# Stick-breaking attention of a two-block model: two heads walked in step, and the sum over later key blocks kept as one

## The chip, the cores and the metric

The kernel runs on one core of a Trainium2 chip. The metric is the device time of one launch in microseconds (us), the median over runs. Four engines do the arithmetic, each with a queue of its own that it works through strictly in the order in which the program wrote it: TensorE (PE) multiplies matrices, VectorE (DVE) and ScalarE (ACT) work element by element and read PE's results from PSUM, GpSimd (POOL) works on SBUF. They wait for one another by semaphores.

## The reference

Two transformer-like blocks run one behind the other on 512 tokens of width 1024 (528 in the second, which puts 16 meta tokens in front). The change touches only the mixer of the second block. That mixer has two halves which share nothing but their input and output projections.

The first half is stick-breaking attention with 8 heads of width 64. Positions are padded to 640, five key blocks of 128:

```
z = q·k * scale
log_keep = where(valid, -softplus(z), 0)            # valid: key before query
log_rest = sum of log_keep over the later keys, own key excluded
attn = where(valid, exp(log_sigmoid(z) + log_rest), 0);  out = attn @ v
```

The second half is a delta-rule recurrence with 8 heads of width 64: S = S·diag(w) + sa(kk·a)^T + v k^T, y = S r. The kernel evaluates it in 9 chunks of 64 positions. Each chunk needs a triangular inverse of its own, and then a step that depends on the state of the chunk before.

## The kernel before, in words

Both halves run interleaved. In the kernel each engine's part is a set of Python generators; at every `yield` another generator may write its next instructions, and `alternate(...)` decides the order. So the order on each engine is fixed when the program is written. A step of a generator is called a tick here.

**The recurrence** is the generator `rk`. It has `rw_prepare(n)` (products of the chunk, L865 and L873, transposes L878/L879, then the inverse: some 14 small steps of 64x64 matmuls, L596 and L615, each answered by a copy or an addition on DVE or ACT of about 0.4 us) and `rw_scan(n)` (L897/L898 "r", L906 "x", L914 "sd", L919/L923 "y"). Two prepares and one scan are under way at a time, in three turns. On PE `rk` has 250 ticks in all (counted from the code).

In "r", the product AR·SB (128 rows, 64 columns of weights, L897) and the product MM·V0 (L898) are added in PSUM. V0 is a tile with 128 rows: its upper 64 rows are zero and its lower 64 rows are the chunk's values, which POOL copies there from SV (L2219) for each of the 9 chunks. The copy waits for every mask and product of POOL before it, and POOL's later operations wait for the copy.

**The attention** is `heads(b)`, once for b = 0 and once for b = 1; each works on 4 heads (i = 0 to 3). The two halves of the partitions, rows 0 to 63 and rows 64 to 127, hold the heads of b = 0 and of b = 1. For each head it walks the key blocks j = 4, 3, 2, 1, 0, whose query widths are `LEN` = 128, 256, 384, 512, 512 (x counts them 0 to 4). For one block:

- PE: z = KA·QA, one fp32 matmul with 64 rows (L938; each fp32 matmul is two records in the profile)
- ACT: abs, exp, ln (L2003, L2005, L2007)
- DVE: softplus as max(z, 0) + ln (L1538); the block at j = 0 is also multiplied by a mask of the padding (L1543)
- POOL: zero above the diagonal (L2098)
- ACT: the negated value, rounded to fp32r, into `KHI` at the block's own place (L2011); DVE: what rounding left over, into `KLO` (L1546)
- PE: into the same PSUM bank add `TRIR` times this block and `ONER` times every block with a larger j, each for the high and the low part (L947). So a head's five blocks have 2, 4, 6, 8 and 10 of these matmuls
- ACT: exp, which gives the attention weights (L2015); POOL: mask (L2098)

After five blocks PE multiplies the weights by V (L955, 5 matmuls with 128 rows and 64 columns, two records each), and ACT copies the result (L2018).

One head takes 26 ticks of `heads(b)` (104 for four heads). The order is `alternate(rk, heads(0), rk, later_by(2, heads(1)))`: in each round two ticks of `rk` and one of each `heads`. DVE and ACT also run `attention_parts()`, which after `ATT_TICKS` rounds prepares the attention's result for the output projection.

After the last of both halves SP loads the first four weights of the output projection and reloads the residual (XSAVE) and the bonus term (BON). The group norm and the output projection (L489) follow.

Of the kernel before, what the change touches and what calls it, by code (L numbers as in the profile page):

```python
# [15 lines left out]
NCH = 9  # L16
ATT_TICKS = 107
# [129 lines left out]
def program(nc, xT, metaT, cols, consts, slabs, lup, gup, out):  # L147
# [137 lines left out]
    V0 = sbuf("V0", [128, 8, 64], st=m4)  # L285
# [87 lines left out]
    rz = steps("rz", "v0", "sb")  # L373
# [4 lines left out]
    rv0 = count("rv0")  # L378
# [9 lines left out]
    hg = [steps(f"hg{i}", "mask", "emask") for i in range(2)]  # L388
    cat2_hi, cat2_lo = count("cat2_hi"), count("cat2_lo")
# [37 lines left out]
    BLOCKS = (4, 3, 2, 1, 0)  # L427
    KHI = [HH[:, a:a + 4, :].rearrange("p k t -> p (k t)") for a in (0, 4)]
# [48 lines left out]
    def tensor():  # L477
# [407 lines left out]
        def rw_scan(n):  # L885
            e, t = n % 2, n // 2
            te.wait_ge(*rv0.at(n))
            if n:
                te.wait_ge(*qd.at("w1", n - 1))
                if n > 1:  # L890
                    te.wait_ge(*qm.at(n - 2))
            else:
                te.wait_ge(*rz.at("sb"))
# [23 lines left out]
            if n:  # L917
                for i in range(4):
                    te.matmul(PS[:, 6, 64 * i:64 * i + 64], SB[:, i, :, :].rearrange("p a t -> p (a t)"),  # L919
                              AR[:, i, n, 1, :], start=True, stop=True)  # L920
                    for par in range(2):
                        h = 2 * i + par
                        ins = te.matmul(PS[64 * par:64 * par + 64, 6, 64 * i:64 * i + 64], SV[e][:, h, :],  # L923
                                        MM[e][:, h, 64:128], start=False, stop=True, skip_group_check=True)
                ins.then_inc(*qy.up(n - 1))
            yield

        def heads(b):
            pb = 64 * b
            for i in range(4):  # L930
                h = 2 * i + b
                for x, j in enumerate(BLOCKS):
                    r, n = 5 * i + x, LEN[j]
                    if x:
                        te.wait_ge(*ha[b].at("att", r - 1))
                    elif i:
                        te.wait_ge(*hs[b].at(i - 1))
                    te.matmul(PS[:, b, 0:n], KA[pb:pb + 64, i, 128 * j:128 * j + 128], QA[pb:pb + 64, i, 512 - n:512],  # L938
                              start=True, stop=True).then_inc(*hp[b].up("z", r))
                    yield  # L940
                    yield
                    yield
                    te.wait_ge(*hd[b].at("lo", r))
                    for q in range(4, j - 1, -1):
                        w = TRIR if q == j else ONER
                        for part in (KHI[b], KLO[b]):
                            ins = te.matmul(PS[:, b, n - LEN[q]:n], w[:, :], part[:, OFF[q]:OFF[q] + LEN[q]],  # L947
                                            start=False, stop=True, skip_group_check=True)
                    ins.then_inc(*hp[b].up("c", r))
                    yield  # L950
                    yield
                te.wait_ge(*ha[b].at("att", 5 * i + 4))
                te.wait_ge(*hg[b].at("emask", 4 * i + 3))
                for j in range(5):
                    ins = te.matmul(PS[pb:pb + 64, b, 512 - LEN[j]:512], VT[:, j, 64 * h:64 * h + 64],  # L955
                                    ATT[b][:, OFF[j]:OFF[j] + LEN[j]], start=(j == 0), stop=(j == 4))
                ins.then_inc(*ho[b].up(i))
                yield

        te.wait_ge(*rz.at("v0"))  # L960
# [3 lines left out]
        rk = pipeline(NCH, rw_prepare, rw_scan)  # L964
        alternate(rk, heads(0), rk, later_by(2, heads(1)))
# [46 lines left out]
    def vector():  # L1012
# [518 lines left out]
        def heads(b):  # L1531
            for i in range(4):
                for x, j in enumerate(BLOCKS):
                    r, n = 5 * i + x, LEN[j]
                    t = TT[b][r % 2]
                    yield
                    ve.wait_ge(*ha[b].at("ln", r))
                    ve.scalar_tensor_tensor(t[:, 0:n], PS[:, b, 0:n], 0.0, t[:, 0:n], ALU.max,  # L1538
                                            ALU.add).then_inc(*hd[b].up("m", r))
                    if j == 0:  # L1540
                        ve.wait_ge(*hd[b].at("m", r))
                        ve.wait_ge(*fz.at("pm"))
                        ve.tensor_scalar(t[:, 0:n], t[:, 0:n], PM[:, 0:1], None, ALU.mult).then_inc(*hm[b].up(i))  # L1543
                    yield
                    ve.wait_ge(*ha[b].at("hi", r))
                    ve.scalar_tensor_tensor(KLO[b][:, OFF[j]:OFF[j] + n], t[:, 0:n], -1.0,  # L1546
                                            KHI[b][:, OFF[j]:OFF[j] + n].bitcast(f32), ALU.mult,
                                            ALU.subtract).then_inc(*hd[b].up("lo", r))
                    yield
                    yield  # L1550
                    yield
                yield

# [9 lines left out]
        ve.wait_ge(*rz.at("v0"))  # L1563
        ve.wait_ge(*rz.at("sb"))
        for s in s_bs:
            ve.wait_ge(s, 16)
        rk = pipeline(NCH, rw_prepare, rw_scan)
        alternate(rk, heads(0), rk, later_by(2, heads(1)), attention_parts())
# [42 lines left out]
    def scalar():  # L1611
# [382 lines left out]
        def heads(b):  # L1994
            pb, a = 64 * b, ha[b]
            for i in range(4):
                for x, j in enumerate(BLOCKS):
                    r, n = 5 * i + x, LEN[j]
                    t = TT[b][r % 2][:, 0:n]
                    ae.wait_ge(*hp[b].at("z", r))  # L2000
                    if r >= 2:
                        ae.wait_ge(*hd[b].at("lo", r - 2))
                    ae.activation(t, PS[:, b, 0:n], ACT.Abs).then_inc(*a.up("abs", r))  # L2003
                    ae.wait_ge(*a.at("abs", r))
                    ae.activation(t, t, ACT.Exp, scale=-1.0).then_inc(*a.up("exp", r))  # L2005
                    ae.wait_ge(*a.at("exp", r))
                    ae.activation(t, t, ACT.Ln, bias=1.0).then_inc(*a.up("ln", r))  # L2007
                    yield
                    yield
                    ae.wait_ge(*(hg[b].at("mask", 4 * i + x) if j else hm[b].at(i)))  # L2010
                    ae.activation(KHI[b][:, OFF[j]:OFF[j] + n], t, ACT.Copy, scale=-1.0).then_inc(*a.up("hi", r))  # L2011
                    yield
                    yield
                    ae.wait_ge(*hp[b].at("c", r))
                    ae.activation(ATT[b][:, OFF[j]:OFF[j] + n], PS[:, b, 0:n], ACT.Exp).then_inc(*a.up("att", r))  # L2015
                    yield
                ae.wait_ge(*ho[b].at(i))
                ae.activation(QA[pb:pb + 64, i, :], PS[pb:pb + 64, b, :], ACT.Copy).then_inc(*hs[b].up(i))  # L2018
                yield

# [12 lines left out]
        rk = pipeline(NCH, rw_prepare, rw_scan)  # L2033
        alternate(rk, heads(0), rk, later_by(2, heads(1)), attention_parts())
# [46 lines left out]
    def gpsimd():  # L2081
# [113 lines left out]
        ge.memset(V0[0:64, :, :], 0.0).then_inc(*rz.up("v0"))  # L2195
        ge.memset(SB[:, :, :, :], 0.0).then_inc(*rz.up("sb"))

        def after_copy():
            if rv0.n:
                ge.wait_ge(*rv0.at(rv0.n - 1))  # L2200

        def rw_prepare(n):
# [5 lines left out]
            after_copy()  # L2208
            yield from invert(rinv[e], rd[e], rg[e], t, False)

        def rw_scan(n):
            e, t = n % 2, n // 2
            ge.wait_ge(*ra[e].at("v", t))
            if n:
                ge.wait_ge(*qp.at("r", n - 1))
            for s in hg + rg:
                if s.n:
                    ge.wait_ge(s.sem, s.n)
            ge.tensor_copy(V0[64:128, :, :], SV[e][64:128]).then_inc(*rv0.up(n))  # L2219
# [4 lines left out]
        def heads(b):  # L2224
            for i in range(4):
                for x, j in enumerate(BLOCKS):
                    r = 5 * i + x
                    yield
                    if j:
                        after_copy()  # L2230
                        ge.wait_ge(*hd[b].at("m", r))
                        keep_above(TT[b][r % 2][:, 0:128]).then_inc(*hg[b].up("mask", 4 * i + x))
                    yield
                    yield
                    yield
                    if j:
                        after_copy()
                        ge.wait_ge(*ha[b].at("att", r))
                        keep_above(ATT[b][:, OFF[j]:OFF[j] + 128]).then_inc(*hg[b].up("emask", 4 * i + x))
                    yield  # L2240
                yield

        rk = pipeline(NCH, rw_prepare, rw_scan)
        alternate(rk, heads(0), rk, later_by(2, heads(1)))


# [212 lines left out]
```

## Time and profile before

| | |
|---|---|
| median of 3 runs | 2175.62 us (2174.77 to 2176.39) |
| the profiled execution | 2179.63 us |
| its span | 2178.4 us |
| PE busy in the span | 2005.8 us (92%) |
| DVE, ACT, POOL busy | 789.1, 706.8, 762.8 us |

"Busy" is the time in which an engine has an instruction in it. Matmuls overlap, so for PE the distance from one start to the next says more than the duration. "Granted clock" is the share of TensorE's full 2.4 GHz that the chip allowed; at 0.5 it runs at 1.2 GHz. The mixer of the second block, with the recurrence and the attention, lies between 1428 and 1726 us of the span.

### The profile page before, as it was taken

What the parts mean: (1) busy time and instruction counts of PE and PEld (TensorE: products, weight loads), DVE (VectorE), ACT (ScalarE), POOL (GpSimd) and SP (SyncE); (2) the same over time, 40 slices, a digit from 0 to 9 for tenths busy, and PEclk for the clock granted to TensorE, in tenths of its full rate; (3) what the DMA queues carried; (4) which work ended last, traced back from release to release, by engine and by line L of the source; (5) the groups of instructions that cost most, each with busy time, mean ns of one, the idle gap of its engine ahead of it and who ended that gap; (6) DMA issues with size and microseconds to landing.
All of it is one profiled execution on the core that took longest, in us unless ns stands there. A gap on an engine that the chain in (4) does not pass through costs nothing. (4 is left out here: it accounts for less than half of the span.)

```text
span 2178.4 us, 32154 instructions
## 1 busy us (share of the span) xinstructions
PE 2005.8 (92%) x13960; PEld 1688.1 (77%) x13960; DVE 789.1 (36%) x1065; ACT 706.8 (32%) x1056; POOL 762.8 (35%) x444
## 2 busy tenths in 40 slices
PE   3879988999999999999999888888999789999997
PEld 2657767777888889999999888876666568888885
DVE  5664452232111103444310366643443433344201
ACT  2453221332322323222222323344554333222222
POOL 2322121434444554444445322211111144444453
PEclk9999998999999999999999989998998899999999
DMA  7332221323333232222233412000000222322321
GB/s 270 116 116 97 71 86 30 100 88 131 126 97 91 88 101 88 91 93 89 85 95 93 130 59 63 30 6 2 2 2 2 115 80 87 97 90 94 97 91 64
DMA packets 55659, 182.76 MB, mean 84 GB/s; under 512 B 7488, under 2 KB 7744, under 8 KB 55392
## 3 DMA queue, kind: packets, MB, share of 16 engines
q1 hardware_dynamic: 55520, 180.72, 25.6%
q8 instruction: 110, 1.80, 0.4%
q14 instruction: 29, 0.24, 0.0%
HBM read 175.45 MB, written 5.24 MB: 83 GB/s over the span
## 5 line engine op out<-in xcount | busy, mean ns | idle before, releaser
L2090 POOL TENSOR_TENSOR WL<-RAWS,WH 128x1024 fp32r<-128x1024 f32 (+2 forms) x275 | 650.4, 2368 | 991.8 <-ACT WH L1622 991.8
L489 PE MATMUL PS<-HH,WH 128*128 128x264 f32 (+2 forms) x2184 | 676.8, 352 | 48.5 <-issue 11.9
L489 PE MATMUL PS<-HL,WH 128*128 128x264 f32 (+2 forms) x2184 | 660.0, 345 | 0.0
L489 PE MATMUL PS<-HH,WL 128*128 128x264 f32 (+2 forms) x2184 | 656.3, 342 | 0.0
L489 PEld LDWEIGHTS PS<-HH,WH 128*128 128x128 f32 (+1 forms) x2184 | 382.6, 193 | 117.0 <-issue 35.6
L1622 ACT ACTIVATE WH<-RAWS 128x1024 fp32r<-128x1024 f32 (+2 forms) x275 | 284.1, 1034 | 453.3 <-PE PS L489 405.7
L489 PEld LDWEIGHTS PS<-HL,WH 128*128 128x128 f32 (+1 forms) x2184 | 383.4, 193 | 47.9 <-issue 1.9
L489 PEld LDWEIGHTS PS<-HH,WL 128*128 128x128 f32 (+1 forms) x2184 | 382.4, 192 | 49.0 <-issue 0.4
L489 PE MATMUL PS<-IHf,WH 128*128 128x512 f32 (+1 forms) x704 | 209.4, 338 | 0.0
L489 PE MATMUL PS<-IHf,WL 128*128 128x512 f32 (+1 forms) x704 | 209.3, 338 | 0.0
L489 PE MATMUL PS<-ILf,WH 128*128 128x512 f32 (+1 forms) x704 | 209.2, 338 | 0.0
L1369 DVE TENSOR_TENSOR TMP<-TMP,PS 128x512 f32<-128x512 f32 (+1 forms) x66 | 45.8, 693 | 254.0 <-PE PS L489 246.8
L1889 ACT ACTIVATE IHf<-TMP 128x512 fp32r<-128x512 f32 (+1 forms) x66 | 42.1, 638 | 285.3 <-DVE TMP L1369 285.3
L489 PEld LDWEIGHTS PS<-IHf,WH 128*128 128x128 f32 x704 | 120.5, 188 | 14.9
L489 PEld LDWEIGHTS PS<-ILf,WH 128*128 128x128 f32 x704 | 120.7, 188 | 14.8
L489 PEld LDWEIGHTS PS<-IHf,WL 128*128 128x128 f32 x704 | 120.4, 188 | 14.9
L1364 DVE TENSOR_TENSOR TMP<-TMP,RSTD 128x528 f32<-128x528 f32 (+1 forms) x44 | 104.4, 2374 | 41.2 <-ACT TMP L1885 41.2
L1376 DVE SCALAR_TENSOR_TENSOR X<-PS,X 128x528 f32<-128x528 f32 (+1 forms) x16 | 11.2, 700 | 222.5 <-PE PS L489 222.5
L1357 DVE TENSOR_TENSOR TMP<-PS,RSTD 128x528 f32<-128x528 f32 (+1 forms) x44 | 30.8, 700 | 150.8 <-PE PS L489 150.1
L2106 POOL TENSOR_TENSOR SQA<-SQA,TMP 128x512 f32<-128x512 f32 (+1 forms) x39 | 53.1, 1361 | 90.4 <-ACT TMP L1635 89.7
L1371 DVE TENSOR_TENSOR ILf<-TMP,IHf 128x512 fp32r<-128x512 f32 (+1 forms) x66 | 47.9, 726 | 46.5 <-ACT IHf L1889 46.5
L1635 ACT ACTIVATE TMP<-X 128x512 f32<-128x512 f32 (+1 forms) x42 | 26.2, 628 | 84.8 <-DVE X L1376 35.7
(493 smaller groups left out, 1929.6 us busy)
## 6 DMA issues: line engine op xcount, KB each, us to landing
RAWS<-w_w_in SPq DMA_DIRECT2D x52, 512.0 KB, 4.3
RAWS<-w_ada SPq DMA_DIRECT2D x32, 512.0 KB, 3.6
RAWS<-w_f0g SPq DMA_DIRECT2D x22, 512.0 KB, 3.5
RAWS<-w_f0u SPq DMA_DIRECT2D x22, 512.0 KB, 3.9
RAWS<-w_f1g SPq DMA_DIRECT2D x22, 512.0 KB, 3.6
RAWS<-w_f1u SPq DMA_DIRECT2D x22, 512.0 KB, 3.6
RAWS<-w_f2g SPq DMA_DIRECT2D x22, 512.0 KB, 3.6
RAWS<-w_f2u SPq DMA_DIRECT2D x22, 512.0 KB, 3.6
```

The costliest lines, as they stand in the source:

```text
L489: ins = te.matmul(ps[0:m, q, o:o + b - a] if len(halves) > 1 else ps[0:m, o:o + b - a], w[:, k * m:k * m + m], v[:, k0 + k, a:b], start=fi ...
L1357: ve.tensor_tensor(tv, place(f, 2 * j), r, ALU.mult).then_inc(*ff_g.up("g", FT * (f - 1) + j))
L1364: ve.tensor_tensor(tv, tv, r, ALU.mult).then_inc(*ff_g.up("r", FT * (f - 1) + j))
L1369: ve.tensor_tensor(tv, tv, place(f, 2 * j + 1), ALU.mult).then_inc(*ff_mul.up(FT * f + j))
L1371: ve.tensor_tensor(IL[f][:, j, :], t, IH[f][:, j, :].bitcast(f32), ALU.subtract).then_inc(*ff_lo.up(FT * f + j))
L1376: ve.scalar_tensor_tensor(xv, place(f, 2 * FT + m), 0.5 if f else MOD[:, 40 + m:41 + m], xv, ALU.mult, ALU.add).then_inc(*ff_x.up(8 * f + m))
L1622: ae.activation(WH[s % NS][:, 0:n], RAW[i % NR][:, 0:n], ACT.Copy).then_inc(*w_hi.up(s))
L1635: ae.activation((TMP[k % 3] if k else SQA)[:, 0:n], X[:, k, t0:T2], ACT.Square).then_inc(*n_sq.up(8 * SQUARED[q] + k))
L1889: ae.activation(IH[f][:, j, :], t, ACT.Copy).then_inc(*ff_hi.up(FT * f + j))
L2090: ge.tensor_tensor(WL[s % NS][:, 0:n], RAW[i % NR][:, 0:n], WH[s % NS][:, 0:n].bitcast(f32), ALU.subtract).then_inc(*w_lo.up(s))
L2106: ge.tensor_tensor(SQA[:, 0:n], SQA[:, 0:n], TMP[k % 3][:, 0:n], ALU.add).then_inc(*n_acc.up(added(q, k)[1] - 1))
```

## The change

1. `heads(0)` and `heads(1)` become one generator `heads()`, in which every step is written for b = 0 and then for b = 1. The z matmuls of the two heads stand next to each other, and so do their sums and their products with V, where the two heads alternate matmul by matmul.
2. A block now has ten ticks instead of five: abs at tick 0, exp 1, ln 2, softplus and mask 4, high part 5, low part 6, sums on PE 7, exp 8, mask of the weights 9. With a tick for the product with V a head pair has 51 ticks, 204 in all. The order becomes `alternate(rk, both, rk, both, rk, both, rk)`: four ticks of `rk` to three of `both`. `ATT_TICKS` goes from 107 to 67.
3. The blocks with a larger j are no longer multiplied one by one. POOL adds this block's log_keep to the running sum (three additions per head, 128, 256 and 384 wide), ACT rounds it (`upper_sum`), DVE takes the remainder (`lower_sum`), and PE multiplies that one sum by `ONER`. The five blocks of a head have 2, 4, 4, 4 and 4 such matmuls: 18 instead of 30.
4. V0 and its copy are gone. "r" multiplies MM[64:128] by SV[64:128], the chunk's values where they lie, with 64 rows.
5. In "y" the four matmuls of L919 come first, with the start flag on the first alone, then the eight of L923.

```diff
             for i in range(4):                                  # rw_scan, "r"
                 for par, q in enumerate(HALF):
                     te.matmul(PS[q, 6, 64 * i:64 * i + 64], AR[:, i, n, 0, :], SB[:, i, par, :], start=True, stop=False)
-                    ins = te.matmul(PS[q, 6, 64 * i:64 * i + 64], MM[e][:, 2 * i + par, 0:64], V0[:, 2 * i + par, :],
-                                    start=False, stop=True)
+                    ins = te.matmul(PS[q, 6, 64 * i:64 * i + 64], MM[e][64:128, 2 * i + par, 0:64],
+                                    SV[e][64:128, 2 * i + par, :], start=False, stop=True)
...
                 for i in range(4):                              # rw_scan, "y"
                     te.matmul(PS[:, 6, 64 * i:64 * i + 64], SB[:, i, :, :].rearrange("p a t -> p (a t)"),
-                              AR[:, i, n, 1, :], start=True, stop=True)
-                    for par in range(2):
-                        h = 2 * i + par
-                        ins = te.matmul(... SV[e][:, h, :], MM[e][:, h, 64:128], start=False, stop=True, ...)
+                              AR[:, i, n, 1, :], start=i == 0, stop=False, skip_group_check=True)
+                for h in range(8):
+                    ins = te.matmul(... SV[e][:, h, :], MM[e][:, h, 64:128], start=False, stop=True, ...)
...
+                    for b, q in enumerate(HALF):                # PE, heads
+                        te.matmul(PS[:, b, 0:n], KA[q, i, 128 * j:128 * j + 128], QA[q, i, 512 - n:512], start=True,
+                                  stop=True).then_inc(*hp[b].up("z", r))
+                    for _ in range(7):
+                        yield
+                    for b in range(2):
+                        te.wait_ge(*hd[b].at("lo", r))
                         for part in (KHI[b], KLO[b]):
-                            ins = te.matmul(PS[:, b, n - LEN[q]:n], w[:, :], part[:, OFF[q]:OFF[q] + LEN[q]], ...)
+                            ins = te.matmul(PS[:, b, 0:n], TRIR[:, :], part[:, KAT[x]:KAT[x] + n], ...)
+                        if x:
+                            if x > 1:
+                                te.wait_ge(*hl[b].at(3 * i + x - 2))
+                            m = LEN[j + 1]
+                            for part in (KHI[b], KLO[b]):
+                                ins = te.matmul(PS[:, b, n - m:n], ONER[:, :], part[:, 512:512 + m], ...)
...
                 for j in range(5):
-                    ins = te.matmul(PS[pb:pb + 64, b, 512 - LEN[j]:512], VT[:, j, 64 * h:64 * h + 64], ...)
+                    for b, q in enumerate(HALF):
+                        h = 2 * i + b
+                        ins = te.matmul(PS[q, b, 512 - LEN[j]:512], VT[:, j, 64 * h:64 * h + 64], ...)
...
+        def lower_sum(i, x, b):                                 # DVE
+            n = LEN[BLOCKS[x]]
+            ve.wait_ge(*hh[b].at(3 * i + x - 1))
+            ve.scalar_tensor_tensor(KLO[b][:, 512:512 + n], TT[b][(5 * i + x) % 2][:, 0:n], -1.0, ...)
...
+        def upper_sum(i, x):                                    # ACT, between ln and the high part
+            for b in range(2):
+                ae.wait_ge(*ht[b].at(3 * i + x - 1))
+                ae.activation(KHI[b][:, 512:512 + n], TT[b][r % 2][:, 0:n], ACT.Copy, scale=-1.0)
...
-            ge.tensor_copy(V0[64:128, :, :], SV[e][64:128]).then_inc(*rv0.up(n))
...
+                    if x in (1, 2, 3):                          # POOL, tick 7
+                        for b in range(2):
+                            t = TT[b][r % 2][:, 128:n]
+                            ge.wait_ge(*hd[b].at("lo", r))
+                            ge.tensor_tensor(t, t, TT[b][(r - 1) % 2][:, 0:n - 128], ALU.add)
...
-        alternate(rk, heads(0), rk, later_by(2, heads(1)), attention_parts())
+        alternate(rk, both, rk, both, rk, both, rk, attention_parts())
```

## Rows read from the trace of the kernel before

**Rows 1.** Windows: stretch; time; busy (x count) PE, PEld, DVE, ACT, POOL; clock; DMA.

```profile
1428.00:1684.00 256.00, 235.36 (x3016) 174.04 (x3016) 109.73 (x244) 128.07 (x285) 35.87 (x90) 0.91 0.01 2
1684.00:1726.00 42.00, 33.09 (x534) 28.14 (x533) 16.52 (x37) 8.58 (x19) 2.12 (x4) 0.84 0.01 2
```

**Rows 2.** Chain of waits behind the stage: start, length, what.

```profile
1728.55 12.99 DMA BON<-bsave
...
1750.10 19.96 PE PS L489 x76
```

**Rows 3.** The same chain inside the stage: z matmuls of four widths, one V product.

```profile
1553.26 0.42 PE PS L938 x2
...
1568.11 0.64 PE PS L938 x2
...
1580.93 0.84 PE PS L938 x2
...
1584.97 1.05 PE PS L938 x2
...
1673.88 3.16 PE PS L955 x10
```

**Rows 4.** Timeline of PE, a head's last sum: start, duration, line, shapes.

```profile
1600.49 0.33 PE L947 MATMUL PS<-HH,ONER 128*128 128x128 f32 x1 [0.41 <-DVE HL L1546]
...
1600.76 0.33 PE L947 MATMUL PS<-HH,ONER 128*128 128x256 f32 x1
...
1601.05 0.34 PE L947 MATMUL PS<-HH,ONER 128*128 128x384 f32 x1
...
1601.40 0.40 PE L947 MATMUL PS<-HH,ONER 128*128 128x512 f32 x1
...
1601.87 0.40 PE L947 MATMUL PS<-HH,TRIR 128*128 128x512 f32 x1
```

**Rows 5.** The same timeline, where lines follow one another on PE.

```profile
1602.94 0.63 PE L596 MATMUL PS<-KC,rv1XB 64*64 64x64 f32 x16
1603.41 0.63 PE L596 MATMUL PS<-rv1XB,rv1C 64*64 64x64 f32 x16
1603.97 0.34 PE L897 MATMUL PS<-SB,AR 128*64 128x64 f32 x4
...
1604.95 3.18 PE L955 MATMUL PS<-RAWS,VT 128*64 128x512 f32 x10
...
1612.72 0.69 PE L914 MATMUL PS<-X 128*64 128x64 f32 x16
1613.34 0.43 PE L919 MATMUL PS<-AR,SB 128*128 128x64 f32 x2
1613.70 0.34 PE L923 MATMUL PS<-X 128*64 128x64 f32 x4
1613.97 0.43 PE L919 MATMUL PS<-AR,SB 128*128 128x64 f32 x2
...
1621.54 1.16 PE L865 MATMUL PS<-AR,BK 64*128 64x128 f32 x16
1622.63 0.68 PE L906 MATMUL PS<-RAWS,RX 64*64 64x64 f32 x16
```

**Rows 6.** Groups by line and form, 1428 to 1726: busy, mean ns, idle before.

```profile
L897 PE MATMUL PS<-SB,AR 128*64 128x64 f32 x144 | 10.6, 240 | 2.1 <-DVE SB L1527 1.3 <-POOL V L2219 0.8
...
L1546 DVE SCALAR_TENSOR_TENSOR HL<-TMP,HH 128x512 fp32r<-128x512 f32 x12 | 9.1, 754 | 8.1 <-ACT HH L2011 8.1
...
L1538 DVE SCALAR_TENSOR_TENSOR TMP<-PS,TMP 128x512 f32<-128x512 f32 x12 | 8.2, 687 | 8.5 <-ACT TMP L2007 8.5
...
L2007 ACT ACTIVATE TMP<-TMP 128x512 f32<-128x512 f32 x12 | 7.6, 633 | 0.4
...
L2098 POOL TENSOR_SCALAR_AFFINE_SELECT TMP<-TMP 128x128 f32<-128x128 f32 x24 | 7.1, 297 | 125.0 <-DVE TMP L1538 125.0
```

**Rows 7.** The same view, whole span, POOL: an addition of two tiles.

```profile
L2106 POOL TENSOR_TENSOR SQA<-SQA,TMP 128x512 f32<-128x512 f32 x32 | 43.5, 1358 | 70.5 <-ACT TMP L1635 69.7
```

More of the change, by code:

```diff
@@ L16 @@
 NCH = 9
-ATT_TICKS = 107
+ATT_TICKS = 67
 DELTA_TICKS = 30
@@ L370, in program @@
     at_tr = count("at_tr")
-    rz = steps("rz", "v0", "sb")
+    rz = count("rz")
     rp = [steps(f"rp{i}", "bk", "u", "tr", *INV_PE) for i in range(2)]
@@ L388, in program @@
     hg = [steps(f"hg{i}", "mask", "emask") for i in range(2)]
+    ht, hh, hl = ([count(f"{x}{i}") for i in range(2)] for x in ("ht", "hh", "hl"))
     cat2_hi, cat2_lo = count("cat2_hi"), count("cat2_lo")
@@ new lines, in heads @@
+                    for _ in range(3):
+                        yield
+                for b in range(2):
+                    te.wait_ge(*ha[b].at("att", 5 * i + 4))
+                    te.wait_ge(*hg[b].at("emask", 4 * i + 3))
+                for j in range(5):
+                    for b, q in enumerate(HALF):
+                        h = 2 * i + b
+                        ins = te.matmul(PS[q, b, 512 - LEN[j]:512], VT[:, j, 64 * h:64 * h + 64],
+                                        ATT[b][:, OFF[j]:OFF[j] + LEN[j]], start=(j == 0), stop=(j == 4))
+                        if j == 4:
+                            ins.then_inc(*ho[b].up(i))
@@ L963, in tensor @@
         te.wait_ge(*at_vt.at("t1", 3))
-        rk = pipeline(NCH, rw_prepare, rw_scan)
-        alternate(rk, heads(0), rk, later_by(2, heads(1)))
+        rk, both = pipeline(NCH, rw_prepare, rw_scan), heads()
+        alternate(rk, both, rk, both, rk, both, rk)
         def joined2(k):
@@ L1544, in heads @@
-                    yield
[L1545 to L1551, printed above, removed]
-                yield
+                    for _ in range(4):
+                        yield
@@ L2007, in heads @@
-                    ae.activation(t, t, ACT.Ln, bias=1.0).then_inc(*a.up("ln", r))
+                    t = [TT[b][r % 2][:, 0:n] for b in range(2)]
+                    for b in range(2):
+                        ae.wait_ge(*hp[b].at("z", r))
+                        if x >= 2:
+                            ae.wait_ge(*ht[b].at(3 * i + x - 2))
+                        ae.activation(t[b], PS[:, b, 0:n], ACT.Abs).then_inc(*ha[b].up("abs", r))
+                    yield
+                    for b in range(2):
+                        ae.wait_ge(*ha[b].at("abs", r))
+                        ae.activation(t[b], t[b], ACT.Exp, scale=-1.0).then_inc(*ha[b].up("exp", r))
@@ L2008, in heads @@
+                    yield
+                    for b in range(2):
+                        ae.wait_ge(*ha[b].at("exp", r))
+                        ae.activation(t[b], t[b], ACT.Ln, bias=1.0).then_inc(*ha[b].up("ln", r))
+                    yield
+                    if x in (2, 3, 4):
+                        upper_sum(i, x - 1)
                     yield
                     yield
-                    ae.wait_ge(*(hg[b].at("mask", 4 * i + x) if j else hm[b].at(i)))
-                    ae.activation(KHI[b][:, OFF[j]:OFF[j] + n], t, ACT.Copy, scale=-1.0).then_inc(*a.up("hi", r))
+                    for b in range(2):
+                        ae.wait_ge(*(hg[b].at("mask", 4 * i + x) if j else hm[b].at(i)))
+                        ae.activation(KHI[b][:, KAT[x]:KAT[x] + n], t[b], ACT.Copy, scale=-1.0).then_inc(*ha[b].up("hi", r))
@@ new lines, in heads @@
+                    yield
+                    yield
+                for b, q in enumerate(HALF):
+                    ae.wait_ge(*ho[b].at(i))
+                    ae.activation(QA[q, i, :], PS[q, b, :], ACT.Copy).then_inc(*hs[b].up(i))
+                yield
+        def upper_sum(i, x):
+            r, n = 5 * i + x, LEN[BLOCKS[x]]
+            for b in range(2):
+                ae.wait_ge(*ht[b].at(3 * i + x - 1))
+                ae.activation(KHI[b][:, 512:512 + n], TT[b][r % 2][:, 0:n], ACT.Copy,
+                              scale=-1.0).then_inc(*hh[b].up(3 * i + x - 1))
@@ L2032, in scalar @@
             ae.wait_ge(s, 16)
-        rk = pipeline(NCH, rw_prepare, rw_scan)
-        alternate(rk, heads(0), rk, later_by(2, heads(1)), attention_parts())
+        rk, both = pipeline(NCH, rw_prepare, rw_scan), heads()
+        alternate(rk, both, rk, both, rk, both, rk, attention_parts())
         def group_norm(i):
```

147 lines of the change are left out of this document (65 added, 82 removed).

## The prediction

> **What bounds the kernel now.** The windows come first [rows 1]. While attention and recurrence run together, from 1428 to 1684 us, PE has work in it for 235.4 of 256 us at a granted clock of 0.91; ACT is busy for half of that time, DVE for 43%, POOL for 14%. After 1684 us only the recurrence is left: 42 us with 33.1 us of PE work at a clock of 0.84. So over the stage of 298 us PE is busy 268.5 us and idle 29.5 us. It is the bound for the first 256 us, and a chain of small steps is the bound of the last 42.
>
> The chain of waits shows next what hangs on the end of the stage: the reload of BON takes 12.99 us and the output projection starts at 1750.10 us, 24 us after the last step of the recurrence [rows 2]. SP waits for the last of both halves before it loads, before and after the change, so I carry these 24 us over. What the change is worth is then PE time, plus what the new order does to PE's idle time.
>
> **The prices on PE.** A z matmul takes 0.42, 0.64, 0.84 and 1.05 us for 128, 256, 384 and 512 columns, a V product 3.16 us [rows 3]. In a sum, two matmuls (high and low part) take, start to start, 0.27 us for 128 columns, 0.29 for 256, 0.35 for 384 and 0.47 for 512 [rows 4].
>
> Starts in [rows 5] show two more things. First, matmuls on the two halves of the array overlap: 8 of 128 columns with 64 rows, alternating halves, take 1.09 us (L865), 0.14 us each, where one alone takes 0.42 [rows 3]. Second, a change of the tile's shape costs time. Sixteen records of 64x64 take 0.47 us when the next matmuls have the same shape (1602.94 to 1603.41) and 0.56 us when the next are 128x64 (1603.41 to 1603.97): +0.09 us to leave. L914 (128x64) comes from 64x64 and goes to 128x128 and takes 0.62: about 0.04 more to enter and 0.02 of its own. L897/L898 and L955 share a shape. I take 0.13 us for one change.
>
> **Part by part**, at full clock.
>
> *z matmuls in pairs.* One head costs 0.42 + 0.64 + 0.84 + 2 x 1.05 = 4.0 us, eight heads 32.0 us. Paired as L865's are, the second is free: -16.0 us. Bounds: 0 (no overlap for long matmuls) and -16.0.
>
> *V products in pairs.* 8 x 3.16 = 25.3 us, halved: -12.6 us. Alternating 128x64 tiles are L914's form: 8 products of 64 columns in 0.62 us, 0.08 each, so they overlap too. Bounds 0 and -12.6.
>
> *One sum in place of the later blocks.* A head paid 0.27, 0.56, 0.91, 1.38 and 1.85 us, with 0.09 for leaving each time 5.4 us in all. It now pays 0.27, 0.29 + 0.27, 0.35 + 0.29, 0.47 + 0.35 and 0.47 + 0.47, together 3.23, and half of the leaving (two heads share it), 3.46 us. 8 x 1.96 = -15.7 us. Only columns and shapes enter, so I keep no wide bound here.
>
> *"y" reordered.* A group of L919 and two L923 takes 0.63 us, L919 0.36 of it [rows 5]; four make 2.5 us. Afterwards four L919 in a row, 4 x 0.32, one change and eight products as L914's 0.62: 1.95 us. -0.57 x 8 = -4.6 us.
>
> *"r" without the copy.* Here the edit costs PE time. Now sixteen products, all 128x64, take 0.98 us (1603.97 to 1604.95), because the two halves overlap. Afterwards AR·SB keeps 128 rows and MM·SV has 64, and they alternate: 16 changes of shape at 0.13 us are 2.1 us, and between two changes there is one product of two records and nothing beside it, 16 x 2 x 0.059 = 1.9 us (0.059 is 0.47 over 8). That is 4.0 us for 0.98, +3.0 us in each of 9 chunks: +27.1 us. The trace has no run of this alternation. Bounds: 0 (the change of row count counts for nothing) and +27.1; I take the upper end, since every change of row or column count that [rows 5] show was paid for. In return POOL's copy goes; PE waited 0.8 us for it in L897 [rows 6]: -0.8 us.
>
> The Trainium skill says in "TensorEngine Tiling (Array Packing)", section Tiling Modes, that changing the tiling mode, as opposed to the tile, drains the engine; it names no price. The same page's table of theoretical speedups (section Overview) gives up to a factor of two for a contraction of 64 or less, by which the new MM·SV would be the cheaper form: "r" would stay at 0.98 us or fall, and the 27.1 us would not come. The drain agrees with the 0.56 against 0.47 us; no row here shows the gain for products that all sit in the same half of the rows.
>
> *Sum on PE:* -16.0 - 12.6 - 15.7 - 4.6 + 27.1 - 0.8 = -22.6 us; at the stage's mean clock of 0.90 that is -25 us.
>
> *What moves to the others.* ACT gets 24 roundings of the running sum, at most 0.63 us each (15 us), DVE 24 remainders, at most 0.75 (18 us), POOL 24 additions, each under the 1.36 us of a 512-wide one [rows 6, 7], and loses 9 copies. Over a stage of 270 us ACT comes to about 152 us busy and DVE to 144; neither is the bound. Their cover: `upper_sum` lies on ACT after ln, while two softplus operations (0.69 each) and a mask (0.30) are under way, 1.7 us against its 1.3. Without that cover it would cost up to 15 us. POOL's additions have until the next block's ln. Behind them on POOL wait the mask of the weights, wanted only by the V product, and the inverse's two products.
>
> The trace has the remainder (two SBUF inputs, L1546) at 0.754 us and the softplus (one input in PSUM) at 0.687 [rows 6]. The Trainium skill, "SBUF — State Buffer", section "SBUF: two separate sides", says that a DVE operation with two SBUF inputs and a GpSimd operation that reads SBUF take a shared pair of ports in turns, so the later one waits for the whole of the earlier. The 0.07 us would fit. By the rule each POOL addition could hold one DVE operation, at most 24 times; DVE is half idle, so I leave the sum as it is.
>
> *The chain of a block.* The heads' own chain gets longer, because each engine does the step for both. At 512 columns: z 1.05, six ACT operations 3.8, the second softplus 0.69, mask 0.30, high part 0.63, low part 0.75, sums 0.94, exp 0.63: 8.8 us, and with about ten handovers of 0.05 some 9.3. PE has in that time z, both sums (1.9) and 13.3 ticks of `rk`. In the last 42 us of the stage 42 ticks of `rk` held 33.1 us of PE, 0.66 each at full clock [rows 1]. 13.3 x 0.66 + 1.05 + 1.9 = 11.7 us. PE has more to do than the chain lasts, in the widest block with 2.4 us to spare, so PE stays the bound.
>
> But an answer of ACT or DVE to the recurrence can now stand behind two of the heads' operations instead of one. I add 3 us of new waits, an estimate between 0 and the rival below.
>
> *The tail.* Before, `heads` ended in round 106 and `rk` in round 125 (250 ticks, two a round). Now `rk` ends in round 63 (four a round), `heads` in round 68. The lone tail of the recurrence goes, with about 12 us in which PE waited or ran at half clock. In its place the heads stand alone for 17 ticks: the rest of a block (some 4 us), one of 9.3, a V product of 3.2 and its copies, 1.2, some 18 us with 8 us of PE work. 10 us of idling for 12: I call it 0, bounds -8 and +8.
>
> Altogether -25 + 3 = -22 us: the profiled execution would take 2179.6 - 22 = 2157.6 us. The median before lies 4.0 us under the profiled execution, so 2153.6; I say **2153**.
>
> **Rivals.**
>
> *The alternating shapes cost nothing* ("r" stays at 0.98 us). For it: [rows 5] have no case in which only the row count changes within one bank and the column half stays. Against it: the changes from 64x64 to 128x64 were paid for. -27.1 x 1.1 = -30 on top: 2124.
>
> *The long matmuls do not overlap as those of L865 do.* Then z and V give back 28.6 us, 31 with the clock: 2184. Half of it gives 2169. For it: the trace has no pair of 512 columns. If idle time returns so much that all is used up, the result is 2175, no change.
>
> *Slower: the recurrence waits behind pairs.* `rk` on PE makes 250 / 3 = 83 steps of three ticks. Every step wants an answer of ACT or DVE. Behind a second operation of the heads this comes 0.63 us later. If each step paid half a microsecond that PE can't fill, 42 + 4 us more would be lost: -22 + 46 = +24, 2200. It decides from 22 / 83 = 0.27 us per step on. For it: ACT gets its work in lumps of 1.3 us, "r" is 3 us longer on the chain from one chunk to the next, and PE has fewer matmuls to put in between. Against it: before, with idle time of 21 us in 256 [rows 1], some 70 such steps lost 0.3 us each at most, and a heads' operation already stood ahead of many.
>
> **Chances.** The forecast 0.47 (its own range 2138 to 2168), free shapes 0.20, the returned gain 0.15, the slower case 0.18. Under 0.2% (about 4.4 us, which measurements of this kernel can just tell from none) lies a third of the returned gain and a little of its neighbours. Faster 0.73, same 0.07, slower 0.20. The range takes in the free shapes at 2124 with a little for the tail, and goes up to the middle of the slow case: 2112 to 2190.
>
> **What would show it.** In the profile after: L938 in pairs of 1.05 us at 512 columns; V products of two heads in 3.2 us instead of 6.3; at most 8 records of the sum per head and block; the 16 products of "r" over 4 us instead of 1; "y" in 1.95 us; PE's busy time in the stage down by 20 to 30 us and the attention's last copy as the stage's end, some 276 us after its start. Wrong it would be if "r" kept its 1 us, if two long z matmuls took 2.1, or if PE's idle time in the stage rose by more than 10 us.

## Result and the profile after

The changed kernel takes 2197.03 us (median of 4 runs, 2196.25 to 2201.82), the one before 2176.01 in runs beside it: ratio 1.0103, 95% interval 1.009 to 1.0115. It is 21 us slower; 22 us faster was forecast, and 2197 lies above the range. The profiled execution took 2196.25 us with a span of 2194.9, 16.5 us more than before.

Windows of the changed kernel (columns as in [rows 1]): both halves together, and the heads alone.

```profile
1420.00:1714.00 294.00, 248.76 (x3406) 199.75 (x3408) 123.18 (x283) 122.11 (x301) 49.40 (x100) 0.83 0.01 2
1714.00:1742.00 28.00, 13.45 (x48) 7.35 (x44) 9.87 (x18) 11.34 (x21) 3.82 (x7) 0.61 0.00 0
```

The stage takes 322 us instead of 298. PE is busy 262.2 us, less than before, but idle 59.8 us (29.5 before), and the granted clock is 0.83 and 0.61 where it was 0.91 and 0.84. Busy time times clock gives an estimate of the PE work at full clock: 214.7 us, against 268.45 x 0.90 = 241.6. So PE has 27 us less to do and the stage takes 24 us more. Most of the new idle time lies where both halves run, 45.2 us against 20.6 [rows 1]; the lone end idles 14.6 us against 8.9. The stage starts 8 us earlier than before, because the first 445 us ran at a clock of 0.96 instead of 0.92 in these two executions; the kernels are alike there. In the builds below the stage starts anywhere from 1418.8 to 1428.4 us, so I read differences of a few us from the stage and not from the whole.

The chain of waits of the changed kernel ends the stage with the heads (answers to [rows 2]):

```profile
1731.24 1.22 PE PS L947 x2
1732.46 0.85 PE PS L954 x2
...
1735.90 4.90 PE PS L965 x19
...
1744.66 13.90 DMA BON<-bsave
```

The last pair of V products takes 4.90 us here, mostly at half clock. The recurrence's last "y" had started at 1714.0; for the 27 us after it the heads are alone. From the end of the stage to the end of the span it is 454 us in both kernels.

Timeline of PE in the changed kernel (answers to [rows 3 to 5]; L940 is z, L898/L899 "r", L921/L925 "y", L965 the V product):

```profile
1448.69 1.13 PE L940 MATMUL PS<-QA,KA 64*128 64x512 f32 x4
1449.75 0.68 PE L597 MATMUL PS<-rv1XU,rv1UD 64*64 64x64 f32 x16
...
1452.09 0.33 PE L898 MATMUL PS<-SB,AR 128*64 128x64 f32 x2
1452.35 0.32 PE L899 MATMUL PS<-X 64*64 64x64 f32 x2
1452.60 0.33 PE L898 MATMUL PS<-SB,AR 128*64 128x64 f32 x2
...
1564.10 3.23 PE L965 MATMUL PS<-RAWS,VT 128*64 128x512 f32 x20 [0.73 <-ACT RAWS L2047]
1567.26 0.68 PE L597 MATMUL PS<-rv0LD,rv0UD 64*64 64x64 f32 x16
...
1603.33 1.10 PE L921 MATMUL PS<-AR,SB 128*128 128x64 f32 x8
1604.36 0.69 PE L925 MATMUL PS<-X 128*64 128x64 f32 x16
1604.98 0.33 PE L879 MATMUL PS<-KC,BK 128*128 128x128 f32 x1
```

Two z matmuls of 512 columns take 1.06 us together, two heads' V products 3.16, "y" 1.65, and each single product of "r" 0.26 us, sixteen of them 4.1. These prices of the forecast hold, only "y" is cheaper than its 1.95.

What PE waits for in the sums, from the view of waits of the changed kernel (engine, line, releaser: us in all, times, longest):

```profile
PE PS L947 <- DVE HL L1563: 28.9, 13, 6.9
```

The same wait in the kernel before:

```profile
PE PS L947 <- DVE HL L1546: 3.8, 6, 1.3
```

Not all of the 25 us between them is new idle time. The same view of the changed kernel, first up to the last "y" and then for the heads alone:

```profile
PE PS L947 <- DVE HL L1563: 17.2, 11, 2.8
...
PE PS L947 <- DVE HL L1563: 11.7, 2, 6.9
```

While both halves run, these waits grew by 13.4 us, from 3.8 to 17.2. The other 11.7 us are two waits in the lone end, where PE has nothing of the recurrence left. The second growth, while both halves run, is idle time ahead of the steps of the recurrence's inverse (L597 and L616, before L596 and L615): 19.4 us against 10.7, added up from PE's gaps. One answer that shows it is the recurrence's copy X on ACT, before and after, where both halves run:

```profile
PE PS L596 <- ACT X L1979: 1.6, 2, 1.3
...
PE PS L597 <- ACT X L2001: 5.3, 7, 1.3
```

One wait ahead of the sums in the changed kernel's timeline, at the widest block, and ahead of it a wait of the inverse:

```profile
1552.86 0.62 ACT L2033 ACTIVATE RSTD<-RSTD 128x512 f32<-128x512 f32 x1
...
1552.99 0.69 DVE L1550 SCALAR_TENSOR_TENSOR TMP<-PS,TMP 128x512 f32<-128x512 f32 x1 [1.10 <-ACT TMP L2033]
...
1553.98 0.59 ACT L2001 ACTIVATE X<-PS 64x512 f32<-64x512 f32 x1
...
1554.60 1.15 ACT L2059 ACTIVATE HH<-TMP 128x512 fp32r<-128x512 f32 x2
...
1554.63 0.68 PE L597 MATMUL PS<-KC,SQA 64*64 64x64 f32 x16 [0.57 <-ACT X L2001]
...
1555.66 0.61 ACT L2041 ACTIVATE HH<-TMP 128x512 fp32r<-128x512 f32 x1
...
1556.18 0.61 ACT L2041 ACTIVATE HH<-RSTD 128x512 fp32r<-128x512 f32 x1
1556.24 1.28 DVE L1573 SCALAR_TENSOR_TENSOR HL<-TMP,HH 128x512 fp32r<-128x512 f32 x2
...
1557.44 0.68 DVE L1563 SCALAR_TENSOR_TENSOR HL<-TMP,HH 128x512 fp32r<-128x512 f32 x1
1558.05 0.68 DVE L1563 SCALAR_TENSOR_TENSOR HL<-RSTD,HH 128x512 fp32r<-128x512 f32 x1
...
1558.18 0.62 PE L947 MATMUL PS<-HH,TRIR 128*128 128x512 f32 x1 [2.40 <-DVE HL L1563]
```

The rounding of the running sum (L2059) stands on ACT ahead of the high part (L2041), its remainder (L1573) on DVE ahead of the low part (L1563) for which PE waits 2.40 us. The first head's high part was done at 1556.27, so its low part could have started there; the remainders of both heads put it off to 1557.44, about 1.2 of the 2.40 us. The recurrence's copy X (L2001) stood on ACT behind the ln of both heads (L2033), and PE waited 0.57 us for it.

### The profile page after: what moved, and what is told of

The parts are those of the page before. It is cut to its first block, busy times and chain, and to the rows that moved or that the text cites. A ratio compares the mean times of both kernels' runs of the same rounds, so it can differ in the third digit from the quotient of the medians.

```text
span 2194.9 us, 31965 instructions
## 1 busy us (share of the span) xinstructions
PE 1988.4 (91%) x13864; PEld 1682.1 (77%) x13864; DVE 803.0 (37%) x1089; ACT 705.1 (32%) x1080; POOL 776.7 (35%) x458
## 4 chain that ended last, share of the span: by engine, by line
PE 79%; DVE 11%; ACT 5%; issue 3%; DMA 2%; SPq 0%; POOL 0%; DVEq 0%; ACTq 0%
PE PS L490 64%; PE PS L597 3%; PE PS L947 1%; DMA ADA<-w_ada 1%; DVE TMP L1118 1%; PE PS L940 1%; PE PS L899 1%; PE PS L898 1%; DVE TMP L1115 1%; DVE ACC L1033 1%; PE PS L954 1%; PE PS L965 1%; DMA BON<-bsave 1%; PE PS L866 1%; ACT WH L1644 1%
## 5 line engine op out<-in xcount | busy, mean ns | idle before, releaser
L2139 POOL TENSOR_SCALAR_AFFINE_SELECT TMP<-TMP 128x128 f32<-128x128 f32 x24 | 7.6, 320 | 157.9 <-DVE TMP L1550 157.8
```

## Experiments

Theory S: the alternating tile shapes in "r" make the loss. Theory C: PE waits for chains that the new order and the running sum made longer. "Stage" is the time from the first z matmul to the end of the last V product or "y"; "half" is the time of it at half clock; idle is PE's. All three are read from one profiled execution of each kernel.

| kernel | median us | ratio to before (95%) | stage | half | idle |
|---|---|---|---|---|---|
| before | 2176.01 | | 295.6 | 58 | 29 |
| changed | 2197.03 | 1.0103 (1.009, 1.0115) | 320.9 | 120 | 59 |
| e1 | 2216.42 | 1.0185 (1.0148, 1.0223) | 329.2 | 78 | 28 |
| e2 | 2164.51 | 0.9933 (0.9908, 0.9959) | 282.9 | 79 | 61 |
| e3 | 2193.3 | 1.0076 (1.0054, 1.0097) | 313.5 | 109 | 53 |
| e4 | 2200.75 | 1.0116 (1.0098, 1.0133) | 324.0 | 116 | 51 |
| e5 | 2155.21 | 0.9908 (0.9885, 0.993) | 275.8 | 79 | 54 |
| e6 | 2172.31 | 0.9985 (0.9966, 1.0003) | 291.1 | 43 | 29 |
| e7 | 2132.62 | 0.9815 (0.9777, 0.9852) | 251.9 | 21 | 51 |
| e8 | 2166.58 | 0.9964 (0.9945, 0.9984) | 287.3 | 61 | 61 |
| e9 | 2186.18 | 1.0055 (1.0036, 1.0075) | 302.8 | 82 | 52 |
| e10 | 2125.97 | 0.9771 (0.9755, 0.9787) | 245.8 | 17 | 46 |
| e11 | 2142.84 | 0.9852 (0.9829, 0.9874) | 260.0 | 17 | 50 |
| e13 | 2161.63 | 0.9934 (0.9919, 0.995) | 284.6 | 41 | 30 |
| e14 | 2166.66 | 0.9961 (0.9946, 0.9976) | 292.5 | 72 | 27 |
| e15 | 2146.07 | 0.987 (0.9854, 0.9887) | 263.3 | 38 | 56 |

**e1.** The kernel before, "r" as in the change:

```diff
-                    ins = te.matmul(..., MM[e][:, 2 * i + par, 0:64], V0[:, 2 * i + par, :], ...)
+                    ins = te.matmul(..., MM[e][64:128, 2 * i + par, 0:64], SV[e][64:128, 2 * i + par, :], ...)
```

> The kernel before with one part of the change alone: V0's copy is gone and the second product of "r" reads the chunk's values with 64 rows. Theory S (shapes): the 16 changes of tile shape cost about 3 us in each of 9 chunks, PE is the bound, so +27 us at full clock and some 30 with the granted clock of 0.9: about 2205 us, and "r" measures 4.1 us in the trace. Theory C (chains): what made the changed kernel slow is PE waiting for the heads' pairs; the heads are not paired here, so PE's idle time swallows part of "r" and the time stays at 2176 to 2185 us.

41 us slower, by an interval of 32 to 48; the four executions lie between 2208.07 and 2226.24 us, and the profiled one is the fastest of them. Timeline of PE in e1, where L897 and L898 are the two products:

```profile
1483.99 0.33 PE L897 MATMUL PS<-SB,AR 128*64 128x64 f32 x2
1484.25 0.33 PE L898 MATMUL PS<-X 64*64 64x64 f32 x2
1484.50 0.33 PE L897 MATMUL PS<-SB,AR 128*64 128x64 f32 x2
```

And the windows of e1:

```profile
1423.00:1703.00 280.00, 260.85 (x3028) 191.24 (x3030) 109.10 (x244) 127.72 (x285) 31.40 (x81) 0.90 0.01 2
1703.00:1753.00 50.00, 40.73 (x525) 33.12 (x519) 15.27 (x35) 8.28 (x19) 1.52 (x2) 0.76 0.01 1
```

Against [rows 1] PE is busy 33 us longer and its idle time is the same: S, and C's "idle time swallows it" is refuted for this part. The sixteen products cost 9 x 3.1 = 28 us of this at full clock. The rest goes with the clock: 78 us of the stage at half clock against 58.

**e2.** The changed kernel, the same sixteen products in two runs:

```diff
+            for i in range(4):
+                for par, q in enumerate(HALF):
+                    te.matmul(PS[q, 6, ...], AR[:, i, n, 0, :], SB[:, i, par, :], start=i == 0, stop=False, ...)
+            for i in range(4):
+                for par, q in enumerate(HALF):
+                    ins = te.matmul(PS[q, 6, ...], MM[e][64:128, ...], SV[e][64:128, ...], start=False, stop=True, ...)
```

> The changed kernel with "r" in two runs of one shape: first the eight products with 128 rows, then the eight with 64 rows, same sums. S: "r" falls from 4.1 to about 1.2 us, 9 x 2.9 = 26 us less PE work, about 2170 us. C: PE waits in the sums as before, the saved PE time turns in part into idle time, 2185 to 2192 us.

32.5 us less than the changed kernel, now faster than before: S. Of the 38 us that the stage loses, 9 x 2.8 = 25 are the shorter "r". The rest goes with the clock again, 79 us at half clock instead of 120; PE's idle time does not fall (59 and 61 us). PE's timeline in e2 ("r" is L898 and L902) shows 1.3 us for the sixteen:

```profile
1460.05 0.69 PE L898 MATMUL PS<-SB,AR 128*64 128x64 f32 x16
1460.67 0.68 PE L902 MATMUL PS<-X 64*64 64x64 f32 x16
```

Its windows show that the lone tail of the heads stays, 28 us in which PE is busy for 14.5 us at a clock of 0.57:

```profile
1428.00:1683.00 255.00, 207.07 (x3408) 168.55 (x3408) 122.85 (x283) 121.86 (x301) 49.33 (x100) 0.89 0.01 2
1683.00:1711.00 28.00, 14.46 (x40) 7.51 (x40) 9.87 (x18) 10.36 (x20) 3.81 (x7) 0.57 0.00 0
```

What the alternation does to the clock can be read inside "r". In the changed kernel's sixth "r" the products start 0.26 us apart, and 0.40 us apart after the clock has fallen to half at 1592.5:

```profile
1592.06 0.32 PE L899 MATMUL PS<-X 64*64 64x64 f32 x2
1592.32 0.33 PE L898 MATMUL PS<-SB,AR 128*64 128x64 f32 x2
1592.58 0.47 PE L899 MATMUL PS<-X 64*64 64x64 f32 x2
1592.98 0.47 PE L898 MATMUL PS<-SB,AR 128*64 128x64 f32 x2
```

It is no single case. In the changed kernel the clock fell to half during an "r" or within 1 us behind it for 8 of the 9 "r"; in e1, e3, e4 and e9, which alternate too, for 3, 5, 7 and 6 of 9. In the kernel before and in the ten builds with "r" in its old form or in two runs it happened for 3 of 99.

**e6.** The kernel before with e1's edit and e2's grouping.

> The kernel before without V0's copy, with "r" in two runs of one shape. It splits the +41 us of the ungrouped version in two. Shapes alone: two changes instead of 16, "r" takes about 1.25 us instead of 0.98, no wait for the copy: 2174 to 2178 us. If it is the missing zero rows or the earlier start of "r" that shift the order, most of the +41 stays: 2200 or more.

No difference from before beyond the interval. So the copy is worth next to nothing, and e1's 41 us come with the alternation of shapes: e6 has half clock for 43 us, e1 for 78.

**e3.** The changed kernel, the running sum rounded earlier:

```diff
-                    if x in (2, 3, 4):              # ACT tick 3        -  DVE tick 5: lower_sum
-                        upper_sum(i, x - 1)
...
+                    if x in (1, 2, 3):              # ACT tick 9, after exp  +  DVE tick 2: lower_sum
+                        upper_sum(i, x)
```

> The changed kernel with the rounding of the running sum moved off the chain of a block: ACT rounds it right after the exp of the block before (tick 9), DVE takes the remainder at tick 2, while ACT does abs, exp and ln. Nothing else moves. C: PE's wait for the remainders ahead of the sums, 28.9 us in the changed kernel against 3.8 before, falls by half or more, less half clock follows, about 2180 us. S: that wait only stands where PE would have been idle anyway, 2195 us or more.

The waits ahead of the sums fell from 28.9 to 21.1 us, the stage by 7.4, the time by 4, with intervals that overlap a little: between the two theories, less than C said.

**e4.** The changed kernel without the running sum: `KAT` is each block's own place again, and the additions, `upper_sum` and `lower_sum` are gone.

```diff
-                            for part in (KHI[b], KLO[b]):
-                                ins = te.matmul(PS[:, b, n - m:n], ONER[:, :], part[:, 512:512 + m], ...)
+                        for k in range(j + 1, 5):
+                            for part in (KHI[b], KLO[b]):
+                                ins = te.matmul(PS[:, b, n - LEN[k]:n], ONER[:, :], part[:, OFF[k]:OFF[k] + LEN[k]], ...)
```

> The changed kernel in its lock step, but with the later blocks multiplied one by one as before: no additions on POOL, no rounding of the sum on ACT, no remainder of it on DVE, 30 instead of 18 matmuls per head. PE has 15.7 us more to do. C in the form 'the running sum's rounding stands on the chain': PE's wait ahead of the sums falls from 28.9 to under 15 us and the time is about 2190. C in the form 'the lock step itself is too long a chain': the wait stays over 20 us and the time is about 2210. S alone says 2197 + 17 = 2214.

The wait fell to 21.9 us, as in e3, so the sum's conversions cost some 7 us of waiting; with 15.7 us more matmuls the time rose by only 4, again with intervals that overlap. The other 22 us of waiting come with the two heads walked in step, and 10.0 of them lie in the lone end: neither form of C alone.

**e5.** e2 and e3 together.

> The changed kernel with both edits: "r" in two runs of one shape, and the running sum rounded ahead of the block that uses it. Alone they gave -33 and -4 us. If PE's waits ahead of the sums (30.3 us with "r" grouped) are the next bound, the second edit is worth more here than alone, about -10: 2155 us. If the waits are the recurrence's own answers that stand in front of the heads' on DVE and ACT, it is worth 4 us again: 2160.

9 us less than e2, and PE's wait in the sums 21.0 us for 30.3.

**e8.** e2 with the V products of the two heads one after the other.

```diff
-                for j in range(5):
-                    for b, q in enumerate(HALF):
+                for b, q in enumerate(HALF):
+                    for j in range(5):
```

> The changed kernel with "r" grouped and with the V products of the two heads one after the other (no alternation), so PE has about 12.6 us more to do in four places. If PE is still the bound, +12 us over the 2164.5 of the grouped version: 2177. If chains bound the stage, what stands on the heads' chain counts alone: each V product is waited for by the next head's z, four times 3.2 us, also +12; but the pairs' second half is then free to overlap with nothing. If alternating the halves gives no overlap for 512 columns, 0.

Two V products one after the other take 5.6 us instead of 3.2, so PE got 4 x 2.4 = 10 us more to do and not 12.6:

```profile
1485.50 5.64 PE L968 MATMUL PS<-RAWS,VT 128*64 128x512 f32 x20
1491.08 0.68 PE L597 MATMUL PS<-rv0LD,rv0UD 64*64 64x64 f32 x16
```

They gave 2 us of time, which the intervals do not separate from none, and 4.4 of stage. That does not show that the work went into idle time: PE idles 61 us in both. What fell is half clock, from 79 to 61 us, which hides up to 9 us of the added work. So e8 does not decide between the bounds.

**e7.** e5 with another order of the ticks on all four engines (the interleave).

```diff
-        alternate(rk, both, rk, both, rk, both, rk)
+        alternate(*[(rk, both)[c == "b"] for c in "rrbrbrbrbrrbrbrbrbrb"])      # ATT_TICKS = 22
```

> The version with both edits, and eleven ticks of the recurrence to nine of the heads instead of four to three, so that both end in the same round. With four to three the heads stand alone for the last 28 us of the stage (2682.8 is not meant: last y at 1682.8, last V product at 1710.5 us). If that tail is idle time that can be filled, about 10 us less than with four to three: 2146 us. If PE's waits only move into the mixed part, the same time within 3 us.

22.6 us less than e5, 24 in the stage. The lone end of 27 us is down to 3. PE idles only 3 us less, so most of the gain is the clock: 21 us at half clock instead of 79.

**e9.** The changed kernel with e7's interleave alone.

> The changed kernel with nothing but the interleave altered, eleven ticks of the recurrence to nine of the heads. With both edits it gave 22 us. If the lone end of the heads is what costs (26 us from the last y to the last V product in the changed kernel), it gives 20 to 25 us here too: about 2174. If it only pays once "r" is short, because a chain through "r" sets the mixed part, 5 us or less: 2192.

11 us less, 18 in the stage: half of the first forecast. The order pays with the long "r" as well, and more without it.

**e10 and e15.** e5 at seven to six and at ten to nine.

```diff
-        alternate(rk, both, rk, both, rk, both, rk)
+        alternate(*[(rk, both)[c == "b"] for c in "rrbrbrbrbrbrb"])             # e10, ATT_TICKS = 34
+        alternate(*[(rk, both)[c == "b"] for c in "rrbrbrbrbrbrbrbrbrb"])       # e15, ATT_TICKS = 22
```

> The version with both edits, seven ticks of the recurrence to six of the heads (3.5 to 3), so that the recurrence ends about two rounds of the old count after the heads. If 22 us came from ending together, this is 3 to 8 us slower than eleven to nine (2132.6): 2138. If fewer ticks of the recurrence per round are better in themselves, because less stands ahead of the heads' operations, it is as fast or faster: 2132 or less.

> The version with both edits, ten ticks of the recurrence to nine of the heads (3.33 to 3), the next step past seven to six. The recurrence would now end about one and a half outer rounds after the heads. If ending together is what counts, it is slower than 2126: 2132 or more. If fewer ticks of the recurrence ahead of the heads' operations are what counts, 2122 or less.

Seven to six is the best version here, 50 us (2.3%) under the kernel before; one step further loses 20. All four executions of e10 are faster than the fastest of e7. So neither the fewest ticks of the recurrence ahead of the heads nor the exact tie is best. In e15 the last V product is at 1669.8 and the last "y" at 1687.0, a lone tail on the other side. Windows of e10:

```profile
1423.00:1658.00 235.00, 191.18 (x3245) 154.44 (x3243) 127.36 (x291) 128.78 (x315) 53.02 (x106) 0.96 0.01 2
1658.00:1669.00 11.00, 8.23 (x190) 7.05 (x186) 2.92 (x7) 3.22 (x8) 0.00 (x0) 1.00 0.01 1
```

Its wait in the sums, from the view of waits:

```profile
PE PS L951 <- DVE HL L1569: 16.2, 17, 3.6
```

**e11.** e7 without the running sum, as in e4.

> Grouped "r", eleven to nine, and the later blocks multiplied one by one as before (no running sum). It prices the running sum where PE has idle time: PE has 15.7 us more to do, DVE and ACT 24 operations less each. In the changed kernel taking it out cost 4 us. If PE work is hidden in idle time, within 4 us of 2132.6; if it now counts in full, about 2148.

10 us slower than e7, 8 in the stage: here the running sum pays for about half to two thirds of its 15.7 us, where e4 against the changed kernel gave 4. The executions of the two overlap (e7 2128.55 to 2145.94, e11 2139.71 to 2149.27), so the size is rough.

**e13 and e14.** The kernel before with "y" in the change's order (e13), and the same together with e6 (e14).

```diff
-                for i in range(4): ... AR product of i, then the two SV products of i
+                for i in range(4): ... AR product of i, start=i == 0
+                for h in range(8): ... SV product of h
```

> The kernel before with "y" in two runs of one shape and nothing else. By the prices of the forecast 0.57 us less in each of 8 chunks on a busy PE: 2176 - 5 = 2171 us. If "y" hides behind other work: 2176.

> The kernel before (heads unpaired, no running sum, its own order) with the recurrence's part of the change in its cheap form: no copy, grouped "r", reordered "y". Alone the two gave -2 and -15 us, so 2160 us. Then pairing, finer steps and running sum at four to three, which end at 2164.5 in the grouped version, are worth +5 us at that order, and -34 us at seven to six. If the two overlap (the order of the recurrence shifts), 2170 or more.

e13 is 15 us faster, 11 in the stage, where 5 were expected. e14 is 9 us faster and 3 in the stage, less than e13 alone, so these two do not add up. In the profiles e14 idles 3 us less than e13 but is busy 11 us longer, at half clock for 72 us against 41; why the clock is lower there stays open. Against e14 the grouped version e2 gains 2 us by the medians and 10 by the stage: pairing, finer steps and running sum together were worth little at four to three, and 41 at seven to six with the early rounding.

## Why the prediction was wrong

*The prices on PE* were right. z and V pairs overlap fully at 512 columns, "r" rose to 4.1 us (4.0 forecast), "y" fell to 1.65 (1.95). The sum was -22.6 us at full clock, -24 with the measured "r" and "y"; the windows give -27.

*The step that failed* is "PE has more to do than the chain lasts ... so PE stays the bound", and with it "I add 3 us of new waits". Idle time rose by 30 us, 25 of them while both halves ran. Two things were wrong with that step. First, the chain was added up without the running sum. Its remainder stands on DVE between the high and the low part, and its rounding on ACT ahead of the high part; I said that the softplus and the mask cover it. With the 1.15 and 1.28 us that the timeline shows for them, the chain of 9.3 us becomes 11.7, and the 2.4 us to spare are gone. e3 and e5 price this at 4 to 9 us. Second, I averaged: 13.3 ticks at 0.66 us assume that the recurrence has work ready, while its own steps wait for DVE and ACT behind pairs. The trace shows it in the idle time ahead of the inverse's steps, 19.4 us instead of 10.7. No run changed only this, so that the pairs cause it is argued from the timeline and not shown.

*The forecast fails without the alternation too.* Leaving out its 30 us gave 2124, as the rival has it. e2, where "r" is 1.3 us, takes 2164.5, still 40 us more. So the miss is in idle time and clock and not in the price of "r".

*"The clock of 0.90" carried over* was wrong too. Time at half clock went from 58 to 120 us, and 41 of these 62 us go again in e2. At 0.82, the clock of the windows weighted by busy time, instead of 0.90 the 214.7 us of work take 262 instead of 239 us. So: -27 / 0.90 = -30 for the work, +23 for the clock, +30 for idling, +23 in all, against 24 measured. This splits the measured times and does not test them: its parts come from the same windows.

*The tail "I call it 0"* was too small. The heads stood alone for 27 us, not 18, at a clock of 0.61. The windows have 14.6 us of idling there, where the lone recurrence had 8.9, so 6 us more and not none, and the half clock comes on top. Letting both end together gave 11 us in the changed kernel (e9) and 22 with both edits (e7). The forecast had counted the rounds and not drawn the conclusion that four to three is past the balance of 250 to 204 ticks.

*"r" at +27.1 us* had the right price on PE (28 measured) and too small an effect: 33 us in the changed kernel, 41 in the kernel before. The difference goes with the half clock during and behind "r", which the forecast didn't have. The rival that its shapes cost nothing is refuted. The rival "slower: the recurrence waits behind pairs", 2200 us, is nearest to the measured time, but by luck: it put 46 us on 83 waits of half a microsecond, and the inverse's steps waited 9 us longer. Removing the alternation alone takes the kernel below the one before.

*The rule on the tiling mode* from the Trainium skill ("TensorEngine Tiling (Array Packing)", Tiling Modes), that a change of mode drains the engine, agrees with the row of "r": 0.26 us for each product that changes the shape, 0.08 in a run of one shape (L898 in e2). How much of this is the drain and how much the lost overlap of the two column halves, no run separates. The factor of up to two for short contractions in the same page's table (Overview) did not show: the eight products with 64 rows, all in rows 64 to 127, take 0.68 us, the eight with 128 rows 0.69 (L902 and L898 in e2).

## What to carry to other kernels

Keep matmuls of one tile shape together: in a run where two halves of the array alternate, a small fp32 product takes 0.08 us, between two changes of shape 0.26, and the whole loss was larger than this PE time, because the clock fell with it. When an engine that was the bound gets less work, recompute the chain with every operation that stands in front in the queues, the new ones included, and recount in which round each interleaved stream ends: letting the two streams end together gave 11 us in one version and 22 in another, by the clock more than by PE's idle time. And don't carry the clock of the old profile over to an order in which PE idles otherwise.

## What was not expected of the hardware

The granted clock does not follow PE's idle time alone: e1 has 28 us of idling and 78 us at half clock, e7 51 and 21. What it does follow is the alternation in "r": each of the pairs that differ in it alone (e1 and e6, the changed kernel and e2, e3 and e5) has 31 to 41 us more at half clock with it, at an idle time that differs by at most 3 us. Why the clock falls there stays open; no run held the order fixed and changed only what PE did in its waits. Four products with 128 rows and 128 columns of weights in a row (L921) take 1.03 us, 0.26 each, where one between changes of shape took 0.36 [rows 5].
